# Eight modulation loads of a two-block transformer moved from TensorE to GpSimd, and the twenty pairs behind them set closer

## The reference

```python
c_act = jax.nn.silu(c)
mod = c_act @ w_ada[l] + b_ada[l]                      # (2048) x (2048, 12288)
sh1, sc1, gt1, sh2, sc2, gt2 = jnp.split(mod, 6, axis=-1)
h = rms_norm(x, g_norm1) * (1 + sc1) + sh1
proj = h @ w_in                                         # q, k, v of the differential attention; cq, ckv, k_pe
a_out = differential_attention(q_d, k_d, v_d, lam, rel_bias)   # 8 heads: "the first attention"
q_m = rms_norm(cq) @ w_q_b;  kv = rms_norm(ckv) @ w_kv_b       # "the latent stage"
b_out = latent_attention(q_m, k_m, v_m)                 # 8 heads: "the second attention"
x = x + gt1 * (concat(a_out, b_out) @ w_out)
h2 = rms_norm(x, g_norm2) * (1 + sc2) + sh2
x = x + gt2 * ((silu(h2 @ w_gate) * (h2 @ w_up)) @ w_down)
```

## Time and profile before

| | before |
|---|---|
| median of three runs | 2655.3 us |
| the profiled execution | 2656.51 us |
| its span, first to last instruction | 2654.1 us |
| PE busy | 2583.4 us (97%) |
| DVE busy | 1547.0 us (58%) |
| ACT busy | 1166.7 us (44%) |
| POOL busy | 54.3 us (2%) |
| DMA moved | 563.8 MB, mean 212 GB/s |
| granted TensorE clock, mean | 0.991 |

### The profile page before, as it was taken

How to read it: one execution, slowest core, us unless ns; L and a number is a source line. 1 busy time by engine, 2 the same in 40 slices (tenths; PEclk the granted TensorE clock), 3 DMA queues, 4 the chain that set the end, 5 groups by cost and what they waited for, 6 DMA issues and landing times.

```text
span 2654.1 us, 32740 instructions
## 1 busy us (share of the span) xinstructions
PE 2583.4 (97%) x12054; PEld 2074.6 (78%) x12054; DVE 1547.0 (58%) x1698; ACT 1166.7 (44%) x1522; POOL 54.3 (2%) x86
## 2 busy tenths in 40 slices
PE   7999989899999999999999999999999999999997
PEld 2676766688888888887888888888888888888886
DVE  1456664577776555557655454566555656555555
ACT  2344554344444444444544455444544444444443
POOL 1010110000000000000000000000000000000000
PEclk8999999899999999999999999999999999999999
DMA  9968776657776555555655545566555555555552
GB/s 391 384 231 292 261 270 239 229 199 248 250 249 222 191 191 190 191 191 178 211 191 186 177 153 175 186 202 238 188 193 189 190 190 190 190 190 189 188 189 98
DMA packets 263106, 563.80 MB, mean 212 GB/s; under 512 B 9251, under 2 KB 13525, under 8 KB 261869
## 3 DMA queue, kind: packets, MB, share of 16 engines
q1 hardware_dynamic: 260688, 549.25, 61.0%
q0 software_dynamic: 1952, 11.27, 1.2%
q10 hardware_dynamic: 380, 2.13, 0.2%
HBM read 558.40 MB, written 4.21 MB: 212 GB/s over the span
## 4 chain that ended last, share of the span: by engine, by line
PE 83%; DVE 2%; ACT 1%; issue 0%; DMA 0%; POOL 0%; DVEq 0%; POOLq 0%; ACTq 0%
PE acc L635 79%; PE bank L716 2%; PE bank L665 1%; DVE w_lo L1681 0%; PE acc L857 0%; PE acc L909 0%; PE bank L728 0%; PE bank L866 0%; PE acc L855 0%; DMA raw<-in_w_ada 0%; DVE wide L2191 0%; DVE x_res L2195 0%; PE acc L1067 0%; PE acc L1068 0%; DVE actT_hi L1812 0%
## 5 line engine op out<-in xcount | busy, mean ns | idle before, releaser
L1681 DVE TENSOR_TENSOR w_lo<-raw,w_hi 128x1024 fp32r<-128x1024 f32 x852 | 1037.7, 1224 | 831.1 <-ACT w_hi L1153 802.3
L1153 ACT ACTIVATE w_hi<-raw 128x1024 fp32r<-128x1024 f32 x852 | 902.8, 1062 | 1059.0 <-PE acc L635 948.8
L635 PE MATMUL acc<-w_hi,actT_hi 128*128 128x512 f32 (+1 forms) x2112 | 833.7, 395 | 2.0 <-DVE actT_lo L1814 0.8
L635 PE MATMUL acc<-w_hi,actT_lo 128*128 128x512 f32 (+1 forms) x2112 | 821.8, 389 | 0.0
L635 PE MATMUL acc<-w_lo,actT_hi 128*128 128x512 f32 (+1 forms) x2112 | 821.4, 389 | 0.0
L635 PE MATMUL acc<-w_hi,mixT_hi 128*128 128x512 f32 (+1 forms) x1280 | 504.1, 394 | 9.6 <-DVE mixT_lo L1804 5.4
L635 PE MATMUL acc<-w_hi,mixT_lo 128*128 128x512 f32 (+1 forms) x1280 | 497.6, 389 | 0.0
L635 PE MATMUL acc<-w_lo,mixT_hi 128*128 128x512 f32 (+1 forms) x1280 | 497.2, 388 | 0.0
L635 PEld LDWEIGHTS acc<-w_hi,actT_hi 128*128 128x128 f32 x2112 | 397.6, 188 | 108.5 <-issue 21.7
L635 PEld LDWEIGHTS acc<-w_hi,actT_lo 128*128 128x128 f32 x2112 | 397.4, 188 | 82.6
L635 PEld LDWEIGHTS acc<-w_lo,actT_hi 128*128 128x128 f32 x2112 | 397.8, 188 | 79.6 <-issue 1.0
(11 more groups left out here) (275 smaller groups left out, 1066.9 us busy)
## 6 DMA issues: line engine op xcount, KB each, us to landing
raw<-in_w_ff SPq DMA_DIRECT2D x128, 1024.0 KB, 5.1
raw<-in_w_in SPq DMA_DIRECT2D x108, 1024.0 KB, 5.2
raw<-in_w_ada SPq DMA_DIRECT2D x64, 1024.0 KB, 5.2
raw<-in_w_gate SPq DMA_DIRECT2D x44, 1024.0 KB, 5.1
raw<-in_w_up SPq DMA_DIRECT2D x44, 1024.0 KB, 5.1
raw<-in_w_down SPq DMA_DIRECT2D x44, 1024.0 KB, 5.0
early_mix<-in_w_ada SPq DMA_DIRECT2D x16, 1024.0 KB, 8.8
wide<-in_w_ada SPq DMA_DIRECT2D x16, 1024.0 KB, 8.7
```

The lines of the kernel that those rows point to most:

```text
L635: last_mm = pe.matmul(acc[p][:, t, 0:width], act[x][:, k0 + c, t * P:(t + 1) * P], w[:, u % SPL, c * NW:c * NW + width], start=first and c ...
L1153: act.activation(w_hi[:, u % SPL, :], raw[:, ld % RAW, (u % DU) * 1024:(u % DU + 1) * 1024], ACT.Copy) \
L1681: dve.tensor_tensor(w_lo[:, u % SPL, :], raw[:, ld % RAW, (u % DU) * 1024:(u % DU + 1) * 1024], w_hi[:, u % SPL, :].bitcast(F32), ALU.subt ...
```

## The change

The first eight of the 48 late loads (four of sh2, four of sc2) are no longer multiplied on PE. GpSimd multiplies each of a load's four 128x512 pieces by its column of silu(c) and adds them up in a new tile `pool_part` (`products_on_pool`): four tensor_scalar and four tensor_tensor to a load, each waiting for the one before. The load's slot of the ring is free when GpSimd is done with it (`pool_used`). These eight loads stand alone, one behind every second "w" load from w 12 on (units 22 to 50). They are two groups of four loads, and PE turns each sum into columns three units after the last product. Two more groups, of four loads each, complete sh2 and sc2 for these columns on PE. So there are eight groups in place of six. The other 40 loads are 20 pairs, in 24 places instead of 39, from unit 54 to 98.

The core of the diff:

```diff
-GAPS = [0] * 12 + [2 * ((i + 1) * 24 // 39 - i * 24 // 39) for i in range(39)] + [0] * 3
+GAPS = [0] * 12 + [1, 0] * 7 + [1] + [2 * ((i + 1) * 20 // 24 - i * 20 // 24) for i in range(24)] + [0] * 3
-GROUPS = PROLOGUE + [(kind, 8 * pair, 8) for kind, pair in ((3, 0), (4, 0), (3, 1), (4, 1), (2, 0), (2, 1))]
+ON_POOL = [(3, 0, 4), (4, 0, 4)]
+GROUPS = PROLOGUE + ON_POOL + [(3, 4, 4), (4, 4, 4), (3, 8, 8), (4, 8, 8), (2, 0, 8), (2, 8, 8)]
+FIRST_PAIR = NPRO + sum(n for _, _, n in ON_POOL)
...
+def on_pool(a):
+
+    return NPRO <= a < FIRST_PAIR
...
+    events = [("columns", n) for a in products(u - 3) if on_pool(a) for n in completed(a)]
+    events += [("row" if n >= len(GROUPS) or GROUPS[n][0] == 2 else "columns", n)
+               for a in products(u - 2) if not on_pool(a) for n in completed(a)]
...
-                    sem_, m = (lo_ready, DU * count) if before[-1] == "w" else (part_ready, sums_by(NPRO + count - 1))
+                    sem_, m = (lo_ready, DU * count) if before[-1] == "w" else \
+                        (pool_used, count) if on_pool(NPRO + count - 1) else (part_ready, sums_by(NPRO + count - 1))
...
+            def products_on_pool(a):
+
+                g, r = LOAD_OF[a]
+                ld = LOADS_A[a - NPRO]
+                if r == 0 and g > len(PROLOGUE):
+                    pool.wait_ge(mod_ready, g)
+                pool.wait_ge(raw_in[ld % RAW], 16 * (ld // RAW + 1))
+                for c in range(4):
+                    k = 4 * r + c
+                    src = raw[:, ld % RAW, c * NW:(c + 1) * NW]
+                    if k == 0:
+                        link(pool.tensor_scalar(pool_part[:, :], src, ccol[:, k, 0:1], None, ALU.mult))
+                    else:
+                        link(pool.tensor_scalar(src, src, ccol[:, k, 0:1], None, ALU.mult))
+                        link(pool.tensor_tensor(pool_part[:, :], pool_part[:, :], src, ALU.add))
+                pool.sem_inc(pool_used, 1)
+                if r == 3:
+                    pool.sem_inc(pool_summed, 1)
...
             for v in range(-24, 52 + 16):
                 for s in window(v):
                     if s[0] in sizes:
                         inv_rms(*sizes[s[0]])
+                for what, n_ in modulation(v + 24):
+                    if what == "part" and on_pool(n_):
+                        products_on_pool(n_)
```

More of the change, by code:

```diff
@@ L100, in sums_by @@
         return LOAD_OF[a][0] + 1
-    return len(PROLOGUE) + ((a - NPRO) // 2 + 1 if a < WIDE else (WIDE - NPRO) // 2 + a + 1 - WIDE)
+    return len(PROLOGUE) + ((a - FIRST_PAIR) // 2 + 1 if a < WIDE else (WIDE - FIRST_PAIR) // 2 + a + 1 - WIDE)
 def sums_of(n_):
@@ L139, in early @@
         return [LEAD + 1 + v] if 0 <= v < NPRO - LEAD - 1 else []
-    events = [("row" if n >= len(PROLOGUE) + 4 else "columns", n) for a in products(u - 2) for n in completed(a)]
+    events = [("columns", n) for a in products(u - 3) if on_pool(a) for n in completed(a)]
+    events += [("row" if n >= len(GROUPS) or GROUPS[n][0] == 2 else "columns", n)
+               for a in products(u - 2) if not on_pool(a) for n in completed(a)]
     events += [("columns", n) for a in early(u - 1) for n in completed(a)]
@@ L145, in takes_bank @@
 def takes_bank(what, n_):
-    return what != "part" or (NPRO <= n_ < WIDE and n_ % 2 == 0) or (LEAD <= n_ < NPRO and LOAD_OF[n_][1] == 0)
+    return what != "part" or (FIRST_PAIR <= n_ < WIDE and n_ % 2 == 0) or (LEAD <= n_ < NPRO and LOAD_OF[n_][1] == 0)
 def banks_of(u):
@@ L269, in build @@
         sel = sb("sel", [P, 2])
+        with ExitStack() as c1:
+            pool_part = sb("pool_part", [P, NW], F32, c1)
         f_raw = sb("f_raw", [P, DC, H])
@@ L340, in build @@
         part_ready = sem("part_ready")
+        pool_used = sem("pool_used")
+        pool_summed = sem("pool_summed")
         mod_ready = sem("mod_ready")
@@ L672, in part_columns @@
             def part_columns(n_):
-                wide_ = n_ < len(GROUPS) and GROUPS[n_][2] == 8
-                pe.wait_ge(part_ready, L.value("groups", sums_of(n_), 4))
+                wide_ = GROUPS[n_][2] == 8
+                of_pool = GROUPS[n_] in ON_POOL
+                if of_pool:
+                    pe.wait_ge(pool_summed, ON_POOL.index(GROUPS[n_]) + 1)
+                else:
+                    pe.wait_ge(part_ready, sums_of(n_))
+                src = pool_part if of_pool else part
                 b, _ = wait_bank()
@@ L678, in part_columns @@
                     if wide_:
-                        ins = pe.matmul(bank[b][:, 2 * j:2 * j + 2], part[:, j * P:(j + 1) * P], sel[:, :], start=True,
+                        ins = pe.matmul(bank[b][:, 2 * j:2 * j + 2], src[:, j * P:(j + 1) * P], sel[:, :], start=True,
                                         stop=True)
                     else:
-                        ins = pe.matmul(bank[b][:, j:j + 1], part[:, j * P:(j + 1) * P], ones[:, 0:1], start=True,
+                        ins = pe.matmul(bank[b][:, j:j + 1], src[:, j * P:(j + 1) * P], ones[:, 0:1], start=True,
                                         stop=True)
@@ L706, in modulate @@
                 for what, n_ in modulation(L.n["unit"] - 1):
-                    if what != "part" or n_ < WIDE:
+                    if what != "part" or (n_ < WIDE and not on_pool(n_)):
                         {"part": part_sums, "columns": part_columns, "row": part_row}[what](n_)
@@ L1417, in _ @@
             group_sums(3)
-            act.wait_ge(mod_ready, len(PROLOGUE) + 4)
+            act.wait_ge(mod_ready, len(PROLOGUE) + len(ON_POOL) + 4)
             for k in range(2):
@@ L1695, in unit @@
                 for what, n_ in modulation(L.n["unit"] - 1):
+                    if what == "part" and on_pool(n_):
+                        continue
                     {"part": part_sums if n_ < WIDE else part_products, "columns": part_columns, "row": part_row}[what](n_)
@@ L1766, in part_row @@
                         dve.wait_ge(gt1_bias, 16)
-                        at_ = (2 * (n_ - len(PROLOGUE) - 4) + j) * NW
+                        at_ = GROUPS[n_][1] * P + j * NW
                         dst, sums = grow[:, at_:at_ + NW], bank[b][:, :]
```

## The result

| | before | after |
|---|---|---|
| median (runs beside each other) | 2656.7 us (2654.3 to 2660.2, 4 runs) | 2690.8 us (2689.2 to 2692.0, 4 runs) |
| ratio, 95% interval | | 1.0127 [1.0114, 1.0140] |
| units 24 to 54 (first attention) | 123.2 us | 134.8 us |
| units 54 to 77 (latent stage) | 102.3 us | 119.0 us |
| units 77 to 100 | 107.7 us | 114.6 us |

The change costs 34 us. The forecast was 2658 and its range ended at 2673. The stage lengths are differences of the start times of units in PE's timeline, and they are the measure of this whole study: the first attention was to become 12.6 us shorter and became 11.6 longer, the two stages behind it were to become 15.3 us longer and became 23.6 longer. Each is read from one profiled execution.

A forecast was written before the change was run, and what follows sets the result against it. PE, busy for 97% of the span, was taken to bound the kernel. The terms -19.1 + 6.5 + 11.2 + 13.5 - 9.4 gave +2.7 us, 2658 us from the median of 2655.3, range 2646 to 2673.

The forecast's parts named there:

- Term one: First attention: nine pairs at 1.85 us leave PE with 2.4 us of their own waits, -19.1 us.
- Term two: First attention: norms, ring slots and columns queued behind GpSimd's loads of 11 us make PE wait, +6.5 us.
- collisions: GpSimd's products wait 0.9 us where DVE reads two tensors, four hits in eight instructions: 3.6 us a load.
- three places: Stalls behind GpSimd: 2 us at the start, 3.5 near units 34 to 38, 1 at the third head's norm.
- GpSimd as the bound: Rival, first attention: two-input products take 2 us, a load some 16 us, 15 us on top: 2673 us; 13%.
- The port: Rival: DVE's two-input operations also wait for GpSimd's instructions, 16 us of DVE time, +5 us on PE: 2663 us; 20%.
- Terms three to five: Behind the first attention: added PE work +11.2 us, late loads in closer pairs +13.5, idle time filled -9.4.
- Term three: Later stages: five more pairs on PE, +9.3 us, and two more groups of columns, +1.9: +11.2 us.
- Terms four and five: Closer stretch: pairs' loads come late through the ring, +13.5 us; three quarters of PE's latent-stage idle time filled, -9.4.

The follow-up runs named there:

- noprod: The changed kernel with GpSimd's products left out, one tensor_scalar per group standing for them: ratio to before 0.9998.
- memset: The changed kernel with each load's products replaced by 20 GpSimd memsets that read nothing, 11.6 us a load: ratio to before 1.0065.
- memset25: The changed kernel with each load's products replaced by 25 GpSimd memsets that read nothing, 14.5 us a load: ratio to before 1.0133.
- fill: `dve8` with 48 matmuls more on PE that add zeros, placed where PE waited in the latent stage: 2657.05 us, ratio 1.0004.
- ringfree: The changed kernel with a load's ring slot given back once landed, GpSimd's products reading a tile of their own: ratio to before 1.0112.
- half: The changed kernel with only two of each load's four pieces multiplied on GpSimd, 6.6 us a load: ratio to before 1.0009.
- dve8: The changed kernel with the eight loads' products on DVE instead of GpSimd, all sums complete: 2657.4 us, ratio to before 1.0000.

## Why the prediction was wrong

**Term one (-19.1 us) was right.** Pairs and their waits gone from the first attention are -21.0 us in `noprod`.

**Term two (+6.5 us) is the step that failed**, first in the length of a load, at its first factor: "0.55 us for 512" with one input. The slope between 2 and 16 elements of a tensor_scalar was carried to 512, and the memset's 0.53 us was read as agreeing. The memset reads nothing. The product took 1.57 us without a collision. The two-input price (1.1 estimated, 1.27 measured) and the collisions (3.6 us a load estimated, 2.5 measured) were near enough. The load was 14.6 us in place of 11.

It failed in the price of a length too. For 14 us a load the prediction had 15 us, and 14.6 cost 32.6; for 11 it had 6.5, and 11.6 (`memset`) cost 16.7. The prediction took GpSimd to be free of all but the loads and counted three places. It left out the norms, which the same engine must do in the same time, and it gave idle PE time no price in the clock, which took 14.1 of the 32.6 us.

**GpSimd as the bound**, with 13%, named the right mechanism and put it at 14 us a load. Its 16 us a load is a wrong sum (4 x 0.55 + 4 x 2 + 0.8 + 3.6 is 14.6), and by its own rule that is 5 us above the forecast and not 15. So its 2673, though nearest, owes something to luck, and is still 18 us too low.

The norm came late and the transposes of unit 35 waited 3.70 us (3.5 said), but the way was partly another. The wait ended with DVE's queue and not with ACT's copy, which waited 1.19 us for its load, less than before (2.22). The ring's large wait was at unit 48 (7.09 us for ACT, 4.06 for PE), a place that the prediction didn't price.

**The port** held DVE as the rival with 20% said, and with GpSimd's real durations it held for longer. The equal lengths of `memset25` and the changed kernel show that little of it reached PE.

**Terms three to five (+15.3 us) were +23.6.** The windows of units 54 to 77 before and after:

```profile
279.10:381.40 102.30, 88.47 (x554) 66.83 (x552) 69.64 (x137) 60.02 (x183) 18.46 (x31) 0.98 0.74 251
290.10:409.10 119.00, 100.79 (x591) 71.80 (x591) 71.94 (x141) 57.19 (x173) 17.11 (x29) 0.91 0.78 276
```

Term three, PE's own work, was right: units 77 to 100 grew by 6.9 us, for three pairs and a group of columns at 6.5, and in units 54 to 77 two pairs and a group are 4.6. Terms four and five together let PE's idle time in units 54 to 77 grow by 2.7 us (2.3 + 3.3 + 5.5 + 1 - 9.4), and it grew by 4.4 (13.8 to 18.2). That nearness is luck, since both terms were wrong in themselves. The waits were at units 58, 62 and 68, as said. At 62 the wait was for the load (2.3 us of 3.3). At 68 its size was right (5.5 us) and its cause wrong: not the load but the bank that DVE frees behind the copy of unit 66's pair, and then ACT. At 58 there were both. PE's waits for loads, which were to grow by 12.1 us, are 4.9 us in the stage where they were 3.3. And of the waits for ACT and DVE little was filled, because the pairs go through the same two banks, and the sum has to be copied by the same DVE (argued, not shown). What the sum left out is the clock: PE's busy time grew by 12.3 us, 4.6 of them are work, and the other 7.7 go with the lower clock, 0.91 in place of 0.98. `fill` shows that this isn't a loss that can simply be had back.

**What is open.** What in the chain of DVE's queue, ACT's queue and the banks holds the 10 us that are left with quarter loads was not tried. Nor was a version in which the norms pass the products on GpSimd, so how the first attention's loss divides among the norms, the columns and the ring is open beyond what `ringfree` says. How much of the 14.1 us that the clock took in the first attention would come back if it were held wasn't tried either; the latent stage says little.

## What to carry to other kernels

A price for an engine that the trace does not show in that form has to be bounded by an instruction of the same form and size; a write-only one is no bound for one that reads. Before work is put on an engine that is idle, add up all that it has to do in the time of one turn, small norms included, and leave room: here full was at 11.6 us a load, and the loss was 2 us at 6.6, 17 at 11.6 and 32 at 14.5. And work that is moved out of one stage must be followed to where it lands: `noprod`, `half` and `dve8` gained 19 to 21 us in the first attention, and each gave it back behind unit 54.

## What the runs showed of the hardware that was not expected

A tensor_scalar of 128x512 in float32 with a scalar for each partition takes 1.57 us on GpSimd when nothing hinders it, more than the tensor_tensor of that size (1.27 us); a memset takes 0.53. The same product on VectorE is 0.48 us, and 0.75 us with the sum fused into it. A VectorE instruction of 128x2 elements with two tensor inputs took 1.21 us beside a GpSimd instruction that reads, and 0.22 beside memsets. Not every GpSimd instruction that reads holds VectorE for its whole length: before and after the change, all fifteen `w_lo` subtractions that began 0.39 us or more behind the start of GpSimd's power (the second instruction of a norm) took 1.21 to 1.23 us, though the power was still running when they began.
